# A third Strassen pair in the double block of an output projection, with its helpers' work in another order

## The reference, cut to what matters

```python
merged = jax.nn.sigmoid(gate_a) * (y_a @ p_a) + jax.nn.sigmoid(gate_b) * (y_b @ p_b)
x = x + merged @ w_out                                     # 256 x 2048 by 2048 x 2048
x = x + cross_attend(rms_norm(x, g_cross), rms_norm(mem, g_mem), ...)   # k, v from the 256 memory tokens
x = x + conv_glu_ffn(rms_norm(x, g_ffn), ...)
```

## Time and profile before

| | us |
|---|---|
| median of 3 runs | 1723.69 (1723.48 to 1723.93) |
| the profiled execution, its own time | 1723.7 |
| its span in the trace | 1721.9 |
| TensorE busy | 1715.3 |
| VectorE busy | 1323.4 |
| ScalarE busy | 991.9 |

### The profile page before, as it was taken

The page is one execution under the profiler, slowest core; times in us unless marked ns, Lnnn a source line. Parts: engine busy times, 40 slices in busy tenths (PEclk is TensorE's granted clock), DMA queues, the critical chain, the costliest instruction groups (busy, mean ns, idle before and its releaser), DMA issues.

```text
span 1721.9 us, 25542 instructions
## 1 busy us (share of the span) xinstructions
PE 1715.3 (100%) x8646; PEld 1458.0 (85%) x8646; DVE 1323.4 (77%) x1832; ACT 991.9 (58%) x1336; POOL 9.9 (1%) x22
## 2 busy tenths in 40 slices
PE   9999999999999999999999999999999999999999
PEld 7888888888888888888888888888888888888887
DVE  6788876667778888887786667777777777799888
ACT  7765655657854444555665565555555555566454
POOL 0000000000000000000000000000000000000000
PEclk9999999999999999999999999999999999999999
DMA  8556565554456566666755455555555555665665
GB/s 325 186 173 185 169 171 174 174 173 148 160 181 197 196 199 196 214 195 222 293 191 189 147 171 195 184 190 186 187 190 186 191 187 188 201 202 189 201 211 176
DMA packets 90970, 331.06 MB, mean 192 GB/s; under 512 B 10224, under 2 KB 10480, under 8 KB 89872
## 3 DMA queue, kind: packets, MB, share of 16 engines
q1 hardware_dynamic: 89424, 321.96, 56.6%
q0 software_dynamic: 1472, 8.12, 2.5%
HBM read 326.83 MB, written 2.10 MB: 191 GB/s over the span
## 4 chain that ended last, share of the span: by engine, by line
PE 99%; DMA 0%; DVE 0%; SPq 0%; ACT 0%; issue 0%
PE ps L437 22%; PE ps L440 11%; PE ps L654 11%; PE ps L655 11%; PE ps L656 11%; PE ps L418 8%; PE ps L420 8%; PE ps L419 8%; PE ps L540 1%; PE ps L541 1%; PE ps L539 1%; PE ps L584 1%; PE ps L583 1%; PE ps L753 0%; PE ps L598 0%; PE ps L591 0%
## 5 line engine op out<-in xcount | busy, mean ns | idle before, releaser
L1550 DVE TENSOR_TENSOR w_lo<-w_raw,w_hi 128x1024 fp32r<-128x1024 f32 x482 | 583.9, 1222 | 285.7 <-ACT w_hi L956 284.7
L956 ACT ACTIVATE w_hi<-w_raw 128x1024 fp32r<-128x1024 f32 x482 | 503.4, 1056 | 351.0 <-PE ps L440 150.3
L437 PE MATMUL ps<-u,w_hi 128*128 128x512 f32 x1664 | 580.8, 395 | 0.0
L440 PE MATMUL ps<-u,w_lo 128*128 128x256 f32 x1664 | 462.0, 278 | 0.0
L437 PEld LDWEIGHTS ps<-u,w_hi 128*128 128x128 f32 x1664 | 312.1, 188 | 72.2
L440 PEld LDWEIGHTS ps<-u,w_lo 128*128 128x128 f32 x1664 | 312.6, 188 | 0.2
L418 PE MATMUL ps<-w_hi,u 128*128 128x512 f32 x416 | 165.8, 399 | 1.5 <-DVE w_lo L1582 1.5
L420 PE MATMUL ps<-w_hi,u 128*128 128x512 f32 x416 | 162.5, 391 | 0.0
L419 PE MATMUL ps<-w_lo,u 128*128 128x512 f32 x416 | 162.1, 390 | 0.0
L656 PE MATMUL ps<-w_hi,h_lo 128*128 128x512 f32 x256 | 99.6, 389 | 0.0
L418 PEld LDWEIGHTS ps<-w_hi,u 128*128 128x128 f32 x416 | 78.2, 188 | 17.5 <-DVE u L1577 1.9
(11 more groups left out here) (545 smaller groups left out, 2941.4 us busy)
## 6 DMA issues: line engine op xcount, KB each, us to landing
w_raw<-in_stream SPq DMA_DIRECT2D x600, 512.0 KB, 3.4
x_tok<-in_x SPq DMA_DIRECT2D x2, 1024.0 KB, 8.3
mem_raw<-in_mem_by_feature POOLq DMA_DIRECT2D x2, 1024.0 KB, 7.0
x_tok<-in_x POOLq DMA_DIRECT2D x2, 1024.0 KB, 8.5
mem_tok<-in_mem POOLq DMA_DIRECT2D x2, 1024.0 KB, 15.0
x_t<-in_x_t SPq DMA_DIRECT2D x7, 256.0 KB, 4.7
w_raw<-in_stream SPq DMA_DIRECT2D x4, 256.0 KB, 5.0
m_st<-ncm POOLq DMA_DIRECT2D x8, 128.0 KB, 6.4
```

Source lines behind the costliest of these rows:

```text
L437: pe.matmul(ps[:, bank + m, :], w_hi[:, s, lo:lo + P], act[:, kc, :, :].rearrange("p h t -> p (h t)"), start=(kc == 0), stop=False)
L440: mm = pe.matmul(ps[:, bank + m, T:2 * T], w_lo[:, s, lo:lo + P], act[:, kc, 0, :], start=False, stop=(kc == KC - 1))
L956: act.activation(w_hi[:, s, :], w_raw[:, s, :], ACT.Copy).then_inc(hi_made, 1)
L1550: TTo(w_lo[:, s, :], w_raw[:, s, :], w_hi[:, s, :].bitcast(F32), ALU.subtract).then_inc(lo_made, 1)
```

## The change

It makes three edits that belong together.

1. `WFAST = (2, 4, 6)`: pair 2 of the double block becomes a Strassen pair. Its form needs buffers of its own (`wn_hi_b`, `wn_sum_b`, `wn_lo_b`). The forms are now made in single block 0 (the first, as before), in single block 1 at chunk 0 (the second, as before) and in single block 1 at chunk 2 (the third, new), where the low part of the form before is made ahead of the sums.
2. `WEXTRA = (4, 5, 0, 1)`: the first two extra products go to banks 4 and 5. Banks 0 and 1 still hold block 1 when the first Strassen pair begins, so the wait for `x1_lo` 8 stands inside the pair, ahead of e7. The transposes of block 1 move from pair 2 to pair 1 on TensorE, with `block_hi` and `block_lo`; block 1's squares and a square root move one pair back on ScalarE.
3. `MEM_AT`: two of the eight memory pieces move forward into single block 0 (chunks 6 and 7), four stand in single block 1 (which had four), two stay in the double block (which had four).

```diff
-WFAST = (4, 6)
+WFAST = (2, 4, 6)
-WMAIN, WEXTRA = (2, 3, 6, 7), (0, 1, 4, 5)
+WMAIN, WEXTRA = (2, 3, 6, 7), (4, 5, 0, 1)
...
-        MEM_AT = {1: {1: 0, 3: 1, 5: 2, 7: 3}, 2: {0: 4, 1: 5, 3: 6, 5: 7}}
+        MEM_AT = {0: {6: 0, 7: 1}, 1: {1: 2, 3: 3, 5: 4, 7: 5}, 2: {3: 6, 5: 7}}
...
                 three(e5, *form(N5), *sums(0), begin, end)
+                if x1_read:
+                    pe.wait_ge(sem("x1_lo"), x1_read)
                 three(e7, *form(N7), *sums(1), begin, end)
...
             for p in range(KPB):
-                if p == 2:
+                if p == 1:
                     block_T("x1", 1, wout_bank(1))
-                if p == WFAST[0]:
-                    pe.wait_ge(sem("x1_lo"), 8)
...
@@ ScalarE, single block 0 @@
             for c in range(3, KPB):
                 split(Pos(G_WOUT), c)
                 if c == 5:
                     wide_form_high(0)
+                if c in MEM_AT[0]:
+                    mem_high(MEM_AT[0][c])
             for c in range(KPB):
                 split(Pos(G_WOUTS[1]), c)
                 if c in MEM_AT[1]:
                     mem_high(MEM_AT[1][c])
-                if c == 0:
-                    wide_form_high(1)
+                if c in (0, 2):
+                    wide_form_high(c // 2 + 1)
...
@@ ScalarE, double block @@
                 if p == 0:
+                    block_hi("x1", 1, wout_bank(1), "g_cross")
+                if p == 1:
                     block_squares("x1", 1, 40)
                     act.wait_ge(sem("norm_mv"), 2)
                     act.activation(tiny[:, 4:6], tiny[:, 2:4], ACT.Sqrt).then_inc(sem("norm_rt"), 1)
-                if p == 1:
-                    block_hi("x1", 1, wout_bank(1), "g_cross")
...
@@ VectorE, single block 0 @@
                 if c == 5:
                     wide_form_sums(0)
+                if c in MEM_AT[0]:
+                    mem_low(MEM_AT[0][c])
                 if c == 7:
                     wide_form_low(0)
             TTo(g_ckq, col("g_cq"), col("g_ck"), ALU.mult)
             x1_add(0)
             for c in range(KPB):
                 split(Pos(G_WOUTS[1]), c)
-                if c == 0:
-                    wide_form_sums(1)
+                if c in (2, 4):
+                    wide_form_low(c // 2)
+                if c in (0, 2):
+                    wide_form_sums(c // 2 + 1)
                 if c in MEM_AT[1]:
                     mem_low(MEM_AT[1][c])
-                if c == 2:
-                    wide_form_low(1)
...
@@ VectorE, double block @@
-                if p == 2:
-                    block_lo("x1", 1, wout_bank(1), "g_cross")
                 if p + 2 in WFAST:
                     g, done = G_WIDE + 2 * (p + 2), MSUMS + WFAST.index(p + 2)
                     fast_sums(g, done, wu_sum)
                     fast_lows(g, done, wu_sum, wu_hi, wu_lo)
+                    if p == 0:
+                        block_lo("x1", 1, wout_bank(1), "g_cross")
```

More of the change, by code:

```diff
@@ L161, in build @@
         wn_hi, wn_sum, wn_lo = nr["wn_hi"], nr["wn_sum"], nr["wn_lo"]
+        nr = region("n_rd", 2048, [("wn_sum_b", [P, 1, BLK], F32)], [("wn_lo_b", [P, 1, BLK], F32R)])
+        wn_sum_b, wn_lo_b = nr["wn_sum_b"], nr["wn_lo_b"]
         w_raw = sb("w_raw", [P, SLOTS, 1024])
@@ L220, in build @@
              ("x_tok", [P, TT, D], F32), ("x_sq", [P, TT, BLK], F32)],
-            [("wn_pad", [P, 13312], F32), ("wn_raw", [P, 2, T], F32)],
+            [("wn_pad", [P, 13312], F32), ("wn_raw", [P, 2, T], F32), ("wn_hi_b", [P, 1, BLK], F32R)],
             [("ua", [P, 4, T], F32), ("ub", [P, 4, T], F32), ("xa", [P, 4, T], F32), ("xb", [P, 4, T], F32)],
@@ L227, in build @@
         (x0_t, x0_tok, lat_tok, kpx, zi8, zf8, g8a, g8b, v_aug, qk, kpe, ncm, cos_g, sin_g, gq, gk, gp, q_tok,
-         k_tok, pe_n, pe_tok, pe_b, v_pair, pr, prt, r0_bc, sig, k_st, w_ml, w_ml_hi, v_st, junk, v_low, w_low, hn, mg_t, nm_hi, nm_sum, pa, n_raw, um_sum, um_hi, nm_lo, um_lo, x_sq, yc, x_tok, wn_raw, ua, ub, xa, xb, u_sum, r_diag, r_bc, n_sum_a, h_hi_c, u_lo, h_hi_a, n_lo_a) = (
+         k_tok, pe_n, pe_tok, pe_b, v_pair, pr, prt, r0_bc, sig, k_st, w_ml, w_ml_hi, v_st, junk, v_low, w_low, hn, mg_t, nm_hi, nm_sum, pa, n_raw, um_sum, um_hi, nm_lo, um_lo, x_sq, yc, x_tok, wn_raw, wn_hi_b, ua, ub, xa, xb, u_sum, r_diag, r_bc, n_sum_a, h_hi_c, u_lo, h_hi_a, n_lo_a) = (
             zz[n] for n in ("x0_t", "x0_tok", "lat_tok", "kpx", "zi8", "zf8", "g8a", "g8b", "v_aug", "qk", "kpe",
@@ L232, in build @@
                             "sig", "k_st", "w_ml", "w_ml_hi", "v_st", "junk", "v_low", "w_low", "hn", "mg_t", "nm_hi", "nm_sum", "pa", "n_raw", "um_sum", "um_hi", "nm_lo", "um_lo", "x_sq", "yc",
-                            "x_tok", "wn_raw", "ua", "ub", "xa", "xb", "u_sum", "r_diag", "r_bc", "n_sum_a",
+                            "x_tok", "wn_raw", "wn_hi_b", "ua", "ub", "xa", "xb", "u_sum", "r_diag", "r_bc", "n_sum_a",
                             "h_hi_c", "u_lo", "h_hi_a", "n_lo_a"))
@@ L284, in m_form, with w_form @@
                 nu_hi[:, i - 4, :], nu_sum[:, i - 4, :], nu_lo[:, i - 4, :])
+        def w_form(i):
+            return (wn_hi[:, i, :], wn_sum[:, i, :], wn_lo[:, i, :]) if i < 2 else (
+                wn_hi_b[:, 0, :], wn_sum_b[:, 0, :], wn_lo_b[:, 0, :])
         def m_fast(n):
@@ L656, in three, with fast_pair @@
                 return pe.matmul(o, a_lo, b_hi, start=False, stop=last)
-            def fast_pair(g, done, form_no, act_part, form, sums, main, extra, begin, end):
+            def fast_pair(g, done, form_no, act_part, form, sums, main, extra, begin, end, x1_read=0):
                 s0, s1 = g % SLOTS, (g + 1) % SLOTS
@@ L786, in wide_fast @@
                 i = WFAST.index(p)
+                hi, raw, lo = w_form(i)
                 fast_pair(G_WIDE + 2 * p, MSUMS + i, MFORMS + i,
                           lambda k, rows: tuple(mg_t[:, 2 * p + k, half, rows] for half in range(2)),
-                          lambda part: (wn_hi[:, i, part], wn_lo[:, i, part]),
+                          lambda part: (hi[:, part], lo[:, part]),
                           lambda m: (wu_hi[:, m, :], wu_lo[:, m, :]),
-                          lambda c: WMAIN[c], lambda c: WEXTRA[c], i == 0, i == len(WFAST) - 1)
+                          lambda c: WMAIN[c], lambda c: WEXTRA[c], i == 0, i == len(WFAST) - 1, 8 if i == 0 else 0)
             pe.wait_ge(sem("x1_lo"), 4)
             for p in range(KPB):
-                if p == 2:
+                if p == 1:
                     block_T("x1", 1, wout_bank(1))
-                if p == WFAST[0]:
-                    pe.wait_ge(sem("x1_lo"), 8)
                 if p in WFAST:
@@ L1327, in wide_form_high @@
                 act.wait_ge(sem("n_sums"), 5 * (MFORMS + i) + 5)
-                act.activation(wn_hi[:, i, :], wn_sum[:, i, :], ACT.Copy).then_inc(sem("n_high"), 1)
+                hi, total, lo = w_form(i)
+                act.activation(hi, total, ACT.Copy).then_inc(sem("n_high"), 1)
             for c in range(3, KPB):
@@ L2088, in wide_form_sums @@
             def wide_form_sums(i):
-                f, q, dst = MFORMS + i, WFAST[i], wn_sum[:, i, :]
+                f, q, dst = MFORMS + i, WFAST[i], w_form(i)[1]
                 h1, h2 = wn_raw[:, 0, :], wn_raw[:, 1, :]
@@ L2104, in wide_form_low @@
                 dve.wait_ge(sem("n_high"), MFORMS + i + 1)
-                TTo(wn_lo[:, i, :], wn_sum[:, i, :], wn_hi[:, i, :].bitcast(F32), ALU.subtract
-                    ).then_inc(sem("n_low"), 1)
+                hi, total, lo = w_form(i)
+                TTo(lo, total, hi.bitcast(F32), ALU.subtract).then_inc(sem("n_low"), 1)
             for c in range(3, KPB):
@@ L2143, in _ @@
                     mem_low(MEM_AT[2][p])
-                if p == 1:
+                if p == 3:
                     dve.wait_ge(sem("norm_rt"), 2)
```

## The result

The changed kernel takes 1727.81 us (median of 13 runs, 1727.27 to 1728.56), the kernel before 1723.64 in the same comparison. The ratio is 1.0024, with a 95% interval of 1.0017 to 1.0031: slower by 4.2 us, as forecast (1728.2). The profiled execution took 1728.37 us.

What follows compares the result with a forecast made beforehand. TensorE was taken to bound the kernel, issuing matmuls without waits after the first 9 us. Three new waits less the saved matmuls, 2.60 + 1.38 + 1.25 - 0.68 = +4.55 us, gave 1728.2 us, range 1726.3 to 1731.0.

Steps and rivals of the forecast that it cites:

- Gain: Pair 2 on TensorE takes 21 matmuls for 24; three at 0.227 us save 0.68 us.
- Step 1: VectorE reaches single block 1 late: its next split starts at 838.01 instead of 837.41, 0.60 us late.
- Step 2, wait A: ScalarE, held by the third form's high part, makes chunk 3's 4.91 us late; TensorE waits 2.60 us at chunk 7.
- Step 3, wait B: Ahead of the double block TensorE waits 1.38 us for block 0's low parts, delayed on VectorE.
- Step 4, wait C: Behind pair 0, the moved transposes wait 1.25 us for block 1's additions; lower bound 0.32.
- The release: End of a low part to the matmul it frees, 0.15 us, plus 0.08 for a longer first matmul: 0.23.
- Step 5: In pair 2, block 1's low parts are done at 872.8, the extra product due at 874.1: cover 1.3, no wait.
- R3: Slower still: TensorE's clock falls to 1.2 GHz; one chunk 2.72 us longer gives 1730.9, two 1733.7; chance 0.07.
- R1: Not slower: ScalarE isn't held at chunk 3's high part; 1724.7, or 1723.0 without any wait; chance 0.10 for both.
- R2: Same waits but smaller, VectorE's work finding gaps: wait A under 2.2, wait C at 0.32; 1726.5; chance 0.10.
- R4: The cover of Step 5 fails as well: another 0.5 to 1.5 us, 1729.2; chance 0.06.

Runs made afterwards that it cites:

- e7: In the kept text an extra product of a Strassen pair, not a run; the run so named is e2 with transposes mid pair 1: 1723.70 us, ratio 1.0001.
- e6: Changed kernel with the third form's high part a chunk later, its low part behind block 0's low parts, transposes mid pair 1, memory pieces spread: 1722.93 us.
- e11: Changed kernel with the third form still made but read by nobody, pair 2 staying plain: 1728.90 us, ratio 1.0030.
- e9: The changed kernel itself, unedited, measured a second time: 1728.17 us, ratio 1.0025.
- e3: Changed kernel with the memory pieces back where they were in the kernel before: 1728.01 us, ratio 1.0024.
- e10: Changed kernel with the memory pieces back where they were before, same kernel as e3, measured again: 1728.10 us, ratio 1.0023.
- e1: Changed kernel with the third form's high part one chunk later on ScalarE, behind chunk 3's own high part: 1724.63 us, ratio 1.0005.
- e2: Changed kernel with Strassen pairs 4 and 6 only, no third form; bank order, memory pieces and transposes as changed: 1724.61 us, ratio 1.0005.
- e8: Changed kernel with the third form's high part a chunk later and block 1's transposes in the middle of pair 1: 1723.84 us, ratio 1.0002.
- e5: Changed kernel with block 1's transposes half a pair later, in the middle of pair 1: 1727.68 us, ratio 1.0023.

## Why the prediction was right

The number, the sign and the mechanism held. Step by step:

- **Gain, -0.68:** right. e6 shows -0.68 in the profile, and e11, which lacks it, 0.73 in its median above e9.
- **Step 1, VectorE 0.60 late:** right. The split predicted at 838.01, 7.31 us ahead of block 0's transposes (845.32), starts 7.30 ahead of them in e9 (838.10 and 845.40). In the first profile it is 6.87 ahead, late transfers adding 0.4. As a cost of the kernel it is not settled (e3, e10): the sum took the transfer's landing from one execution of before, and it moves by 2 us from one to the next.
- **Step 2, wait A 2.60:** 2.68 and 2.26 in two profiles, 2.84 and 2.41 from row to row. ScalarE was held 3.68 us, as said; chunk 3's `w_hi` was predicted 6.40 us behind block 0's transposes (851.72) and started 6.39 behind them in e9 (851.79). The first profile, at 851.94, has these 0.4 us more. e1 shows that the place of this one instruction is the cause, and e11 that the third form brings it without the new pair.
- **Step 3, wait B 1.38:** block 0's low parts were to end 12.80 us behind those transposes (858.12), and end 12.78 behind them in e9 (858.18), 13.21 in the first profile. The wait itself shows as 1.0 to 1.1 us where the clock stays up; from row to row it costs 1.38 (e9: 3.79 less 2.41). In the changed kernel's first profile it is swallowed by slow matmuls.
- **Step 4, wait C 1.25:** 1.25 from row to row in e9 (5.04 less 3.79), 0.91 in the first profile. Its lower bound of 0.32 for the transposes alone was too low: e2 has 0.8 to 0.9. That bound took VectorE as undelayed, although step 1 has it 0.60 late; in e2 the additions start 0.83 us later behind block 0's transposes than before (859.40 less 845.27, against 858.62 less 845.32).
- **The release, 0.23:** too large by a tenth. The 0.15 us from VectorE's end to the matmul came from a row of the kernel's start. Here it is 0.05 and 0.06 (in e9: 854.09 to 854.14, 858.18 to 858.24). It counts only once, behind the last wait, and is the 0.09 between 4.55 predicted and 4.46 in e9.
- **Step 5, cover 1.3:** no wait, right. The low parts end at 873.31, predicted 872.8, and TensorE comes to the product e7 at 874.20, so the cover was 0.9 us, not 1.3. It is thin: e8 has 0.2 us of wait there.
- **R3, the clock:** it happened in the first profile, with the sign that was to speak for R3 (0.50 in a window behind 851), and not at the price of +2.7 us that I gave it. So that sign didn't tell R3 from the forecast. The error was to add the slow matmuls to the waits behind them: these end when VectorE is done, whatever TensorE's pace.
- **R1, R2, R4:** in the first profile `w_hi` of chunk 3 came at 851.94, far behind the 849.2 that would have spoken for R1; A was above R2's 2.2 in both profiles and C nowhere near 0.32; the cover of step 5 held against R4.

## What to carry to other kernels

Where the bounding engine never waits, saved work on it is worth its own time at most (0.68 us here), and the helpers' work that buys it has to fit between each row and its due time. Ask of each new instruction on a helper engine what it waits for and what is queued behind it: one 0.54 us operation that had to wait cost 3.2 us ahead of the weights' high part, and none of that one chunk later. When several waits of one engine hang on one queue, their sum is set by the last release of that queue; a loss ahead of it, a slow clock too, is taken off the waits that follow.

## What the runs showed of the hardware that I had not expected

- TensorE's granted clock fell to 0.50 for 6 to 8 matmuls behind waits of 2.7, 2.6 and 2.3 us (first profile of the changed kernel, e11, e5), and stayed at 1.00 behind one of 2.3 in e9 and of 1.9 and 1.3 in e10 and e3. The Trainium skill, "TensorE: Matmul & The Clock Gate", section "HAM oscillation", says that idle gaps in a matmul stream send the clock back; the trace agrees in three executions, and e9 shows that a gap of the same size doesn't always do it.
- The first matmul behind a wait shows 0.50 us for 0.39 and costs about 0.1 us more where the clock stays up: in e9 the next start is 0.35 us behind it at chunk 7 and 0.34 at the double block, in place of 0.23.
- The same 512 KB transfer (for the split at single block 1, chunk 0) freed ScalarE at 837.12 us in one execution of the changed kernel and at 835.47 in the other, 1.65 us apart in one and the same program. What delayed it isn't shown.
